# Attention mixers of a two-block layer stack: pooled-branch and gate chunks multiplied as joint hi/lo products in pairs of PSUM banks

## The reference, cut to what matters

```python
h = rmsnorm(x, ln_mix[l])
z = h @ w_in[l]
u_pool, q, k, v, gate_logits = jnp.split(z, splits, axis=-1)
a = pool_mixer(u_pool, pool_w[l], pool_scale[l]) @ w_pool_branch[l]
q = partial_rope(rmsnorm(q.reshape(B, S, N_Q_HEADS, HEAD_DIM), q_norm[l]), cos, sin)
k = partial_rope(rmsnorm(k.reshape(B, S, N_KV_HEADS, HEAD_DIM), k_norm[l]), cos, sin)
b = swa_sink_attention(q, k, v, sinks[l]) @ w_attn_branch[l]
g_pool, g_attn = jnp.split(jax.nn.sigmoid(gate_logits), N_BRANCHES, axis=-1)
x = x + (g_pool * a + g_attn * b) @ w_out[l]
```

## Time and profile before

| | us |
|---|---|
| median of 3 runs | 2074.68 |
| lowest, highest | 2074.17, 2075.6 |
| profiled execution, its time | 2074.32 |
| profiled execution, its span | 2072.4 |
| PE, DVE, ACT busy | 1843.8, 1014.7, 703.5 |

### The profile page before, as it was taken

The page is one execution under the profiler, slowest core; times in us unless marked ns, Lnnn a source line. Parts: engine busy times, 40 slices in busy tenths (PEclk is TensorE's granted clock), DMA queues, the critical chain, the costliest instruction groups (busy, mean ns, idle before and its releaser), DMA issues.

```text
span 2072.4 us, 31532 instructions
## 1 busy us (share of the span) xinstructions
PE 1843.8 (89%) x13948; PEld 1438.9 (69%) x13948; DVE 1014.7 (49%) x1434; ACT 703.5 (34%) x1049; POOL 39.2 (2%) x46
## 2 busy tenths in 40 slices
PE   9987776676998866677799999999999999999999
PEld 7944433344894433343478889998888888999888
DVE  5722110111672111011158777877777667787666
ACT  6310000000651000000055555655546445465553
POOL 0000000000000000000000003000000000300000
PEclk9999999989999999899899999999999999999999
DMA  9899999999979999999985554545555556445552
GB/s 397 338 415 429 430 430 431 430 429 425 407 323 419 430 430 429 430 431 430 426 326 194 192 207 174 182 170 185 184 204 193 190 183 216 175 160 183 186 195 88
DMA packets 64654, 626.59 MB, mean 302 GB/s; under 512 B 7168, under 2 KB 7296, under 8 KB 14464
## 3 DMA queue, kind: packets, MB, share of 16 engines
q1 hardware_dynamic: 64512, 624.50, 75.6%
HBM read 623.42 MB, written 1.05 MB: 301 GB/s over the span
## 4 chain that ended last, share of the span: by engine, by line
PE 72%; DMA 19%; DVE 4%; ACT 2%; SPq 2%; issue 1%; DVEq 0%; ACTq 0%
PE ps L606 14%; PE ps L609 7%; DMA dense_ring<-in_moe_w_down 7%; PE ps L869 7%; PE ps L550 6%; PE ps L552 6%; PE ps L551 6%; DMA expert_ring_a<-in_moe_w_down 5%; PE ps L860 5%; PE ps L1093 4%; PE ps L1072 4%; DMA work<-in_moe_w_down 3%; PE ps L849 3%; PE ps L885 3%; PE ps L1077 2%; PE ps L1097 2%
## 5 line engine op out<-in xcount | busy, mean ns | idle before, releaser
L1673 DVE TENSOR_TENSOR w_lo<-dense_ring,w_hi 128x1024 fp32r<-128x1024 f32 x398 | 468.9, 1222 | 54.8 <-ACT w_hi L1246 53.7
L1246 ACT CAST w_hi<-dense_ring 128x1024 fp32r<-128x1024 f32 x398 | 397.0, 1048 | 47.2 <-PE ps L552 26.1
L606 PE MATMUL ps<-h_both,w_hi 128*128 128x512 f32 x1344 | 337.3, 393 | 0.8 <-DVE work L2152 0.8
L606 PEld LDWEIGHTS ps<-h_both,w_hi 128*128 128x128 f32 x1344 | 241.8, 189 | 45.5 <-DVE work L2152 2.2
L2019 DVE TENSOR_TENSOR work<-work,ps 128x256 f32<-128x256 f32 x32 | 13.5, 421 | 484.4 <-ACT work L1437 484.4
L609 PEld LDWEIGHTS ps<-h_both,w_lo 128*128 128x128 f32 x1344 | 183.3, 190 | 13.1
L550 PE MATMUL ps<-h_both,w_hi 128*128 128x256 f32 x656 | 188.5, 287 | 0.4 <-DVE h_both L1679 0.3
L609 PE MATMUL ps<-h_both,w_lo 128*128 128x256 f32 x1344 | 187.4, 282 | 0.0
L552 PE MATMUL ps<-h_both,w_lo 128*128 128x256 f32 x656 | 185.6, 283 | 0.0
L551 PE MATMUL ps<-h_both,w_hi 128*128 128x256 f32 x656 | 185.6, 283 | 0.0
L1437 ACT ACTIVATE work<-ps 128x256 f32<-128x256 f32 x32 | 12.3, 384 | 484.6 <-PE ps L860 484.6
(11 more groups left out here) (319 smaller groups left out, 2852.1 us busy)
## 6 DMA issues: line engine op xcount, KB each, us to landing
dense_ring<-in_dense SPq DMA_DIRECT2D x207, 1024.0 KB, 4.9
expert_ring_b<-in_moe_w_up SPq DMA_DIRECT2D x20, 2048.0 KB, 39.9
expert_ring_a<-in_moe_w_gate SPq DMA_DIRECT2D x19, 2048.0 KB, 42.7
expert_ring_a<-in_moe_w_up SPq DMA_DIRECT2D x19, 2048.0 KB, 41.4
dense_ring<-in_moe_w_down SPq DMA_DIRECT2D x17, 2048.0 KB, 35.7
dense_ring<-in_moe_w_gate SPq DMA_DIRECT2D x17, 2048.0 KB, 39.9
expert_ring_b<-in_moe_w_down SPq DMA_DIRECT2D x14, 2048.0 KB, 44.8
dense_ring<-in_moe_w_up SPq DMA_DIRECT2D x14, 2048.0 KB, 40.0
```

The lines of the kernel that those rows point to most:

```text
L606: mm(bank[b + f], w[0][:, f, k, :], h_pairs[:, k, :], start=k == 0, stop=False)
L1246: S.copy(half_of(key, f, 0), tile_of(slot(key), key, f)).then_inc(rounded.up(key, f), 1)
L1673: V.tensor_tensor(half_of(key, f, 1), tile_of(slot(key), key, f), half_of(key, f, 0).bitcast(F32), ALU.subtract).then_inc(remainder.up(key ...
```

## The change

In both attention mixers chunks 3 to 12 go from `tile_products` to `split_products`. Each now takes a pair of whole banks, named by the table `MIX_BANK`, in place of one bank; both are claimed before the chunk's first matmul, and are given back by the event `joined`. For each chunk ACT gets a copy of columns 256 to 511 of the pair into `uT` or `sig` (helper `part`), and DVE an addition of columns 0 to 255 to it (`joined`), after which it scales in place from SBUF. The wait for the pooled edges goes from DVE to ACT. ACT's Square of the heads goes ahead of its first `part`, and at step 10 `part` goes ahead of the pooled copies. The scaling waits for the addition, since the one reads what the other writes.

```diff
--- before.py
+++ after.py
@@ -524,6 +524,7 @@
 
     LAST_Y_BANK, LAST_MX_BANK = (6, 7, 0, 1), (5, 4, 2, 3)
     E_BANK = {s: ((1, 2), (0, 3)) if after_of(s) in ("m0", "m1") else ((0, 1), (2, 3)) for s in STAGES if s[0] == "f"}
+    MIX_BANK = {3: 6, 4: 4, 5: 6, 6: 4, 7: 6, 8: 6, 9: 6, 10: 2, 11: 6, 12: 4}
     PT_BANK = (0, 1, 4, 5, 6, 7)
     BRANCH_BANK = ((2, 3, 0, 1), (4, 5, 6, 7))
 
@@ -1108,7 +1109,7 @@
         def mix(l):
             s = f"m{l}"
             for j in range(13):
-                b = 1 + j if j < 3 else 6 + j % 2
+                b = 1 + j
                 if j < 2:
                     if j == 0:
                         claim(1, acted, "qkv", s, 0)
@@ -1120,8 +1121,9 @@
                     claim(b, acted, "qkv", s, j)
                     token_products((s, j), b, s)
                 else:
-                    claim(b, vec, *(("u", s, j) if j < 5 else ("scaled", s, j)))
-                    tile_products((s, j), b, h_of(s))
+                    for f in range(2):
+                        claim(MIX_BANK[j] + f, vec, "joined", s, j)
+                    split_products((s, j), MIX_BANK[j], s)
                 if j == 7:
                     PE.wait_ge(vec, "rope", s)
                     for tt in range(TT):
@@ -1600,8 +1602,17 @@
         def mix(l):
             s = f"m{l}"
             coming = [(s, j) for j in range(2, 13)] + [(s, "wp", 0), (s, "wp", 1)]
+
+            def part(j):
+                to = uT[:, 2 * (j - 3):2 * (j - 3) + 2, EDGE:] if j < 5 else sig[:, 2 * (j - 5):2 * (j - 5) + 2, :]
+                if j == 3:
+                    ACT.wait_ge(pooled, "edges", s)
+                ACT.wait_ge(products, (s, j), 1)
+                S.copy(to, ps[:, MIX_BANK[j]:MIX_BANK[j] + 2, T:2 * T]).then_inc(acted.up("part", s, j), 1)
+
             for j in range(13):
                 if j == 10:
+                    part(10)
                     for b in range(2):
                         ACT.wait_ge(products, "poolY", s)
                         for g in (2 * b, 2 * b + 1):
@@ -1617,6 +1628,12 @@
                     heads_of(s, j)
                 if j == 11:
                     exps(s, 0)
+                if j == 3:
+                    ACT.wait_ge(acted, "qkv", s, 2)
+                    S.activation(sq.rearrange("p a u c -> p (a u) c"), qk.rearrange("p a u c -> p (a u) c"),
+                                 ACTF.Square).then_inc(acted.up("qk_sq", s), 1)
+                if j >= 3 and j != 10:
+                    part(j)
                 if j == 7:
                     for tt in range(TT):
                         for j0, j1 in ((0, 4), (4, 5)):
@@ -1629,9 +1646,6 @@
                     ACT.wait_ge(vec, "scaled", s, j)
                     S.activation(sig[:, c:c + 2, :], sig[:, c:c + 2, :], ACTF.Tanh, scale=0.5).then_inc(acted.up("sig", s, j), 1)
                 if j == 3:
-                    ACT.wait_ge(acted, "qkv", s, 2)
-                    S.activation(sq.rearrange("p a u c -> p (a u) c"), qk.rearrange("p a u c -> p (a u) c"),
-                                 ACTF.Square).then_inc(acted.up("qk_sq", s), 1)
                     mf = ms.rearrange("p a u -> p (a u)")
                     ACT.wait_ge(vec, "qk_ms", s)
                     S.activation(mf, mf, ACTF.Sqrt).then_inc(acted.up("qk_rms", s), 1)
@@ -2333,17 +2347,12 @@
                     next(past, None)
                 if j == 1:
                     reciprocal_later(s)
-                elif 3 <= j < 5:
-                    b = 6 + j % 2
-                    DVE.wait_ge(products, (s, j), 1)
-                    DVE.wait_ge(pooled, "edges", s)
-                    V.tensor_tensor(uT[:, 2 * (j - 3):2 * (j - 3) + 2, EDGE:], two(bank[b]), over_tiles(rinv), ALU.mult).then_inc(
-                        vec.up("u", s, j), 1)
-                elif j >= 5:
-                    b, c = 6 + j % 2, 2 * (j - 5)
-                    DVE.wait_ge(products, (s, j), 1)
-                    V.tensor_tensor(sig[:, c:c + 2, :], two(bank[b]), over_tiles(rinv), ALU.mult).then_inc(
-                        vec.up("scaled", s, j), 1)
+                elif j >= 3:
+                    to = uT[:, 2 * (j - 3):2 * (j - 3) + 2, EDGE:] if j < 5 else sig[:, 2 * (j - 5):2 * (j - 5) + 2, :]
+                    DVE.wait_ge(acted, "part", s, j)
+                    seq(V.tensor_tensor(to, ps[:, MIX_BANK[j]:MIX_BANK[j] + 2, 0:T], to, ALU.add), "joined", s, j)
+                    V.tensor_tensor(to, to, over_tiles(rinv), ALU.mult).then_inc(
+                        vec.up("u" if j < 5 else "scaled", s, j), 1)
                 if 3 <= j < 6:
                     next(heads_parts)
                     if j == 4:
```

## The result

| | before | after |
|---|---|---|
| median of 4 runs, us | 2074.63 | 2103.52 |
| lowest, highest | 2074.17, 2075.6 | 2102.7, 2105.56 |
| profiled execution, its span | 2072.4 | 2100.8 |

The ratio is 1.0136 (95% interval 1.0124 to 1.0149); the medians lie 28.9 us apart, the changed kernel being the slower one. The forecast was 2098.5 us, in a range of 2091 to 2104.

The account below looks back on a forecast made before the run. PE sets the pace and DVE has no room either; 9.8 us of delay plus 2.3 us of low clock a mixer, over two mixers, adds 24.2 us to 2074.32, giving 2098.5 us, range 2091 to 2104.

Parts of the forecast that it names:

- The matmuls: Half chunks of joint products on PE: 2.80 us in place of 2.88, 3.4 us saved over both mixers.
- ACT and DVE: Added per chunk: ACT copy 0.585 us, DVE addition 0.691 us; scaling from SBUF 0.692 us, the same as from PSUM.
- Chunk 7 and chunk 8: PE waits for DVE's additions to free banks: 2.2 us ahead of chunk 7, 5.2 ahead of chunk 8, which starts 7.6 late.
- The probabilities: Third group of transposed probabilities waits for chunk 12's bank 4: 3.0 us a mixer, 0.8 of it ahead of the branch.
- the walk: PE, ACT and DVE queues carried forward in program order from 1262.36 with profiled durations: 9.8 us later per mixer.
- The sum of the waits: Per mixer: 7.6 us at chunk 8, less 0.85 saved by chunks 8 to 12, plus 3.0 at the probabilities: 9.8 us.
- the stalls are mild: Rival: the pair of banks is free earlier than read, 1 to 4 us a mixer, 2076 to 2086 us; chance 0.05.
- the saving comes out: Rival: DVE keeps up and PE never waits, 2070.9 us; chance 0.04.
- The clock: Behind chunk 8's start PE's granted clock is near 0.6 for 6 us, costing 2.3 us a mixer, between 1.6 and 2.9.
- it gets worse: Rival: the wait ahead of chunk 7 also drops the clock, or DVE slows beside GpSimd's pooling; 2102 to 2108 us; chance 0.12.
- The range: 2091 to 2104 us, taking in the bounds, the rival in which the clock holds, and the near part of the worse one.
- The sum's own bounds: Bounds of the terms over both mixers: 21.6 to 27.0 us added, so 2095.9 to 2101.3 us.

Follow-up runs that it names:

- the added work alone: Changed kernel with ACT's copy and an extra DVE pass kept, but three narrow products in single banks 6 and 7 as before: 2085.17 us (ratio 1.005).
- joining first: Changed kernel with ACT's copy of chunk j ahead of its cast, and DVE's addition ahead of its subtraction, for chunk j + 2: 2102.1 us (ratio 1.0133).

## Why the prediction was right, and where it fell short

- **The matmuls.** Right: 2.79 us for a half chunk (2.80 forecast). That the trace's 11 ns for each k are saved, and not the 2.5 ns that follow from the Trainium skill's "TensorE: Matmul & The Clock Gate" ("Back-to-back issue gap", given there for an isolated matmul), is what the starts of the half chunks show; no median here can tell the two apart.
- **ACT and DVE.** Right: 0.580, 0.685 and 0.692 us.
- **Chunk 7 and chunk 8.** Right in place and releaser: 2.29 us of idle time ahead of chunk 7 (2.2 forecast), and chunk 8 at 1300.24 without the offset (1300.0). Ahead of chunk 8 PE idles 4.58 us and not 5.2, since the slow chunk 7, which the forecast did not have, fills a part of the same wait. The addition of chunk 7 does sit behind a subtraction that waited for ACT.
- **The probabilities.** Right: 0.59 at the branch and 1.97 at the third group, 0.8 and 2.2 in the walk.
- **The sum of the waits.** 9.8 us forecast; 10.1 with the clock held up by dummies. The runs with the parts taken one by one (6.7, 4.9, 6.1, 11.4, 12.9 and 1.9 us a mixer) came within 0.6 of the walk and its clock terms, one of them (the added work alone) partly by luck. The rivals "the stalls are mild" and "the saving comes out" are out.
- **The clock: the term that was too small.** I put 2.3 us a mixer, behind chunk 8 only, and for that one it was right: 2.5. The step that failed is that an idle time of about 2 us would leave the clock alone. The prediction had two of them in its walk, and kept a low clock behind the one ahead of chunk 7 for the rival "it gets worse". That one did bring it down but cost nothing. The one ahead of the third group of probabilities brought it down too, and 1.5 us were lost with nothing to hide them; no sentence of the prediction weighs that one. So a mixer costs 10.1 + 2.5 + 1.5 = 14.1 us, where the forecast had 9.8 + 2.3 = 12.1. Two mixers make 28.2 of the 28.4 us by which the span grew.
- **The range.** The sum's own bounds ended at 2101.3 us, and the median of 2103.52 lies above them. It lies in the range of 2091 to 2104, by half a us, because the range was drawn wider to take in the near part of "it gets worse" (2102 to 2108, given 0.12). That rival's time and its condition, a low clock behind the wait ahead of chunk 7, both came out, but not its account: the loss came from the third group. So place, releaser and size of the waits were foreseen, and that the number still fell in the range is in part luck.

## What to carry to other kernels

When products move from one bank to a pair, go through the claims: ask who empties the last user's bank and where that engine is in its own queue at that moment, not how busy it is on average. A saving of 0.17 us a chunk on the engine that sets the pace cannot pay for 0.7 us on one that has no slack, and a wait of 2 us on TensorE is to be priced with the slow stretch that may stand behind it (1.5 us for the one at the third group here). If such waits can't be avoided, put the bank that comes back last at the end of the list, or keep the engine busy over the wait: the one was worth 6 us here, the other 8.

## What was not expected of the hardware

How short the idle times were behind which the clock was low, though matmuls had run densely at the upper level ahead of them. Behind waits of 2.3 us (chunk 7, both mixers) and 2.0 us (the third group, both) it was at 1.2 GHz for a while; with the order of banks changed, it stayed up behind 1.1 us in both. At 1.8 us it fell in m0 and not in m1, in one and the same run; at 1.7 us, with joining first, in neither. What decides between the two was not looked into and stays open.
